# Two output layers and the second feed-forward layer with a 512-column matmul and halves added on VectorE

## Chip, core and metric

The kernel runs on one core of a Trainium2 chip, in one launch. The metric is the device time of a run in microseconds (us). Three runs of the kernel before took 2256.59, 2255.11 and 2259.27 us; the median is 2256.59 us. Engines are called as in the profile: PE is TensorE's matmul (PEld its weight load), DVE is VectorE, ACT is ScalarE, POOL is GpSimd, SP is SyncE, which issues nearly all DMAs.

## What is computed

Three blocks follow each other on x, with 256 tokens and width 1024, in float32. Cut to what matters:

```
x = x + gt1 * (concat(fourier, recurrent) @ w_out)         # block 1: "out1"
x = x + gt2 * experts(...)                                 # 16 experts, 554 MB of weights
x = x + gate * ((attn + gated unit) @ w_out_2)             # block 2: "out2"
x = x + gate2 * (relu(h @ w_ff1_2)**2 @ w_ff2_2)           # block 2: ff1 (1024 to 4096), ff2 (4096 to 1024)
two layers of block 3, each: in3 (1024 to 4096), attention and convolution, out3 (1024 to 1024)
```

Between these stand norms over the features, whose sums over x must be complete before the next layer's results can be scaled.

## The kernel before, in words

All activations lie feature-major: 128 features on the partitions, 8 chunks of them for width 1024, 256 tokens in the free dimension. A dense layer is a list of blocks; one block is one chunk of 128 output features, summed over all input chunks k in one PSUM bank. For accuracy each float32 product is made of three matmuls in the type float32r: high weight by high input, low weight by high input, high weight by low input (`parts`, line 719). Each has 128 input rows, 128 output features and 256 columns (the tokens), and all three add up in the same 256 columns of the bank. out1 and out2 have 8 blocks of 8 chunks (192 matmuls each), ff2 has 8 blocks of 32 chunks (768 matmuls), which go in 32 steps of 8 chunks, each step with its own slice of weights.

The high and low weights are made on the way, one 128-feature slice ("split", 8 chunks of 128 columns) at a time: ACT copies the slice with rounding into one of four places of w_hi (`high_parts`, line 1232, instruction at line 1243), DVE subtracts it from the original and writes ring_lo (`low_parts`, line 1637, instruction at line 1644). A place of w_hi is free again when PE has finished the step that used it. PE's block waits for the count w_split that DVE raises.

The first unit of a layer (three blocks) is computed with k as the outer loop (`k_outer`, line 724, matmuls at line 736), so that PE can begin when the first chunk of input is split; the three blocks end together. The others run one block after the other (line 785); ff2 has its own loop (line 1195).

The results of out1, out2 and ff2 are taken from PSUM by DVE (`update`, line 1828): one scalar_tensor_tensor per block, X = X + gate * PSUM, which raises the count evacuated. PE waits for this count before it reuses a bank, ACT before it squares or rounds the new X. DVE's program is one list in fixed order. In out1 a turn of it is: update of block i, low part of split i+3, sum of squares (line 1765). In out2: update, low part of split i+3, low part of the new X for the next layer (`raise_low`, line 1773), sum of squares. In ff2 a turn without a result is: low part of split i+3 and, up to turn 23, one piece of the modulation product of 1024 columns (`add_third`, lines 1740 and 1743); turns 9 to 11, 21 to 23, 30 and 31 also have update, raise_low and two sums (lines 1750 or 1753, and 1765). The low part of split i+3 thus stands behind update i, and the last splits of these turns are the first three of the next layer.

`link` on DVE (line 1623) lets an instruction raise a count and makes DVE wait for it before the next one.

Of the kernel before, what the change touches and what calls it, by code (L numbers as in the profile page):

```python
# [10 lines left out]
ALU = mybir.AluOpType  # L11
# [3 lines left out]
P = 128  # L15
T = 256
NT = T // P
D = 1024
# [219 lines left out]
def build(nc, inp, scratch, out):  # L238
# [51 lines left out]
    with ctx:  # L290
# [173 lines left out]
        FF_LO = ff_parts[:, 0:8 * K1].rearrange("p (k t) -> p k t", k=FF // P)  # L464
        FF_HI = ff_parts[:, 8 * K1:16 * K1].rearrange("p (k t) -> p k t", k=FF // P)

        U_HI = u_hi.rearrange("p (k t) -> p k t", k=KD)
        U_LO = u_lo.rearrange("p (k t) -> p k t", k=KD)
        R = rs[:, 0:UCOL]
# [173 lines left out]
        def _(pe):  # L643
# [77 lines left out]

                return (hi, x_hi), (lo, x_hi), (hi, x_lo)

            def k_outer(g, lo, src, first, ready, each, order):

                for it in g["items"]:
                    pe.wait_ge(S("w_split"), it["s"] + 1)
                    if it["b"] >= 4:
                        pe.wait_ge(S("evacuated"), it["free"])
                for n, k in enumerate(order):  # L730
                    pe.wait_ge(S(ready), first + n + 1)
                    for i, it in enumerate(g["items"]):
                        x = [a[:, k, :] for a in src(it)]
                        wl = lo[:, k, it["col"]:it["col"] + P]
                        for j, (w, a) in enumerate(parts(w_hi[:, it["s"] % HI, k, :], wl, *x)):
                            m = pe.matmul(ps[:, it["bank"], 0:a.shape[-1]], w, a, start=(n == 0 and j == 0),  # L736
                                          stop=(n == KD - 1 and j == 2), skip_group_check=True)
                        if n == KD - 1:
                            count(m, "unit_used" if it["last"] else "block_done")
                        each(n, i)  # L740
# [6 lines left out]
                count(m, "block_done")  # L747

            def dense_blocks(units, src, first, after=lambda i: None, ready="x_split", each=lambda k, i: None,
                             order=range(KD)):  # L750


                for gi, g in enumerate(units):
                    lo = slot(g["u"], KD, g["w"], of=ring_lo)
                    if gi == 0:
                        k_outer(g, lo, src, first, ready, each, order)
                        first = None
                        for it in g["items"]:
                            if it["last"]:
                                after(gi)  # L760
                            yield
                        continue
                    for it in g["items"]:
                        if "flip" in it:
                            flip(it, out_by(units, {"v": 11, "vs": 19}[it["flip"]]))
                            yield
                            continue
                        pe.wait_ge(S("w_split"), it["s"] + (2 if it["turned"] else 1))
                        if it["b"] >= 4:
                            pe.wait_ge(S("evacuated"), it["free"])  # L770
                        bank = it["bank"]
                        h = src(it)
                        i = it["s"] % HI
                        for t in range(NT if it["turned"] else 1):
                            for k in range(KD):
                                if it["turned"]:
                                    x = [a[:, k, P * t:P * t + P] for a in h]
                                    for j, (w, a) in enumerate(parts(w_hi[:, i:i + 2, k, :], lo[:, k, :], *x)):
                                        m = pe.matmul(ps[:, bank, 2 * P * t:2 * P * t + 2 * P], a, w,
                                                      start=(k == 0 and j == 0), stop=(k == KD - 1 and j == 2))  # L780
                                else:
# [10 lines left out]
            def dense(units, order=range(KD)):  # L792
                for _ in dense_blocks(units, lambda it: (X_HI, X_LO), split_input(), order=order):
                    pass

            inputs_split = [0]
# [181 lines left out]
            for t in range(NT):  # L978
                m = pe.matmul(ps[:, 4 + t, :], ones, ROOTS[:, HEADS * t:HEADS * t + HEADS, :], start=True, stop=True)
            count(m, "o_spread")  # L980
            dense(out1)


            column_sums(False)
# [184 lines left out]
            for g in proj2:  # L1169
                unit_ready(g["u"])  # L1170
                w = slot(g["u"], 2, 4, g["w"])
                for it in g["items"]:
# [4 lines left out]
                        m = pe.matmul(ps[:, it["b"] % 4, 0:T], w[:, it["src"], k, it["col"]:it["col"] + P],  # L1177
                                      (AO, SGO)[it["src"]][:, k, :], start=(k == 0), stop=(k == 3))
                    count(m, "unit_used" if it["last"] else "block_done")
            dense(out2)  # L1180
            for _ in raised_dense(ff1, False):
                pass
            for i, g in enumerate(ff2):
                for b, u in enumerate(g["us"]):
                    lo = slot(u, KD, g["w"], of=ring_lo)
                    pe.wait_ge(S("ff_split"), KD * (b + 1))
                    for it, (_, s) in zip(g["items"], g["at"][b]):
                        pe.wait_ge(S("w_split"), s + 1)
                        if b == 0:
                            pe.wait_ge(S("evacuated"), it["b"] - 3)  # L1190
                        for k in range(KD):
                            wl = lo[:, k, it["col"]:it["col"] + P]
                            x = FF_HI[:, KD * b + k, :], FF_LO[:, KD * b + k, :]
                            for j, (w, a) in enumerate(parts(w_hi[:, s % HI, k, :], wl, *x)):
                                m = pe.matmul(ps[:, it["b"] % 4, 0:T], w, a, start=(b == 0 and k == 0 and j == 0),  # L1195
                                              stop=(b == FF // D - 1 and k == KD - 1 and j == 2), skip_group_check=True)
                        count(m, plan.splits[s]["done"][0])
                    if 4 * i + b == KD + 1:
                        ada_sum(5, ACC, "third_used", THIRDS * KD)
                    if 4 * i + b == KD + 2:  # L1200
                        turn(5)
# [418 lines left out]
        def _(dve):  # L1620
# [207 lines left out]
            def update(it, gate):  # L1828

                waits(*it["done"])  # L1830
                dve.scalar_tensor_tensor(X[:, it["n"], :], ps[:, it["b"] % 4, 0:T], gate[:, it["n"]:it["n"] + 1],
                                         X[:, it["n"], :], ALU.mult, ALU.add).then_inc(S("evacuated"), 1)

            def residual(units, gate):

# [561 lines left out]
```

## Time and profile before

| what | value |
|---|---|
| runs | 2256.59, 2255.11, 2259.27 us |
| span of the profiled execution | 2251.4 us; no time of its own is given beside the span |
| PE / PEld busy | 1827.7 us (81%) / 1151.7 us (51%) |
| DVE / ACT busy | 798.3 us (35%) / 525.3 us (23%) |
| mean granted TensorE clock | 0.780 |
| chain of waits, by engine | DMA 52%, PE 38%, DVE 7%, issue 1%, ACT 1% |
| out1: 192 matmuls | about 255 to 279 us |
| experts | about 322 to 1586 us |
| out2: 192 matmuls | about 1747 to 1771 us |
| ff1 | about 1773 to 1867 us |
| ff2: 768 matmuls | about 1867 to 1958 us |

The busy shares are means over stages that have different limits. The chain of waits is followed back from the last instruction, and each of its pieces says from when, for how long and which instruction held the end. A clock of 1.00 is 2.4 GHz, 0.50 is 1.2 GHz.

### The profile page before, as it was taken

The page shows a single profiled execution, that of the slowest core. Times are in us where ns is not written, and L with a number is a line of the kernel's source. Part 1 is how long each engine was busy: PE and PEld are TensorE (multiplying, and loading weights), DVE is VectorE, ACT ScalarE, POOL GpSimd, SP SyncE. Part 2 cuts the span into 40 slices and gives each one's busy share as a digit, 9 for nine tenths or more (in the row PEclk, how much of TensorE's full clock was granted, in tenths as well). Part 3 has the DMA queues.
Part 4 walks back from the last instruction along what each step waited for, and adds up shares of the span by engine and source line. Part 5 has one row for each costly group of instructions (what it writes and reads, how often), then busy time and mean ns, then how long its engine had stood idle before and what let it go on. Part 6 is the DMA issues. An engine that isn't in the chain of part 4 may idle for free.

```text
span 2251.4 us, 33931 instructions
## 1 busy us (share of the span) xinstructions
PE 1827.7 (81%) x14864; PEld 1151.7 (51%) x14864; DVE 798.3 (35%) x1237; ACT 525.3 (23%) x857; POOL 52.6 (2%) x85
## 2 busy tenths in 40 slices
PE   5999887777777776677777777667899999999897
PEld 4896752312222221221221222221798999998897
DVE  5666630000000000000000000010775788688777
ACT  2420220000000000000000000000574564365664
POOL 0024000000000000000000000000000000000000
PEclk9999986657656656765665675675899999999998
DMA  9877899999999999999999999999744559853541
GB/s 368 295 283 292 345 410 425 424 426 425 425 426 425 425 426 425 426 426 426 424 426 426 425 426 425 426 425 425 242 152 138 169 177 348 279 169 122 169 132 66
DMA packets 161044, 760.62 MB, mean 338 GB/s; under 512 B 10391, under 2 KB 99223, under 8 KB 109368
## 3 DMA queue, kind: packets, MB, share of 16 engines
q1 hardware_dynamic: 157288, 754.07, 83.9%
q10 hardware_dynamic: 3664, 5.24, 0.7%
q8 instruction: 68, 1.11, 0.2%
q14 instruction: 24, 0.20, 0.0%
HBM read 756.13 MB, written 3.14 MB: 337 GB/s over the span
## 4 chain that ended last, share of the span: by engine, by line
DMA 52%; PE 38%; DVE 7%; issue 1%; ACT 1%; SPq 0%; DVEq 0%; ACTq 0%
DMA arena<-in_w_exp_gate 22%; DMA arena<-in_w_exp_up 21%; PE ps L785 17%; PE ps L1195 4%; DMA ring<-in_w_exp_down 3%; PE ps L1053 3%; PE ps L736 3%; DMA arena<-in_w_ada 2%; PE ps L1067 2%; DMA ring<-in_w_exp_up 2%; PE ps L659 1%; DVE ring_lo L1644 1%; PE ps L1177 1%; PE ps L931 1%; DVE const L2027 1%
## 5 line engine op out<-in xcount | busy, mean ns | idle before, releaser
L1053 PE MATMUL ps<-arena,const 128*32 128x352 f32 x2816 | 409.1, 726 | 162.4 <-DMA arena<-in_w_exp_gate 100.7
L1053 PEld LDWEIGHTS ps<-arena,const 128*32 128x32 f32 x2816 | 99.1, 148 | 460.0 <-DMA arena<-in_w_exp_gate 181.3
L1644 DVE TENSOR_TENSOR ring_lo<-ring,w_hi 128x1024 fp32r<-128x1024 f32 x220 | 267.4, 1219 | 45.8 <-ACT w_hi L1243 44.8
L785 PE MATMUL ps<-u_hi,w_hi 128*128 128x258 f32 x960 | 275.5, 287 | 1.3 <-DVE ring_lo L1644 1.1
L2025 DVE TENSOR_TENSOR tail<-tail,ps 128x704 f32<-128x704 f32 x15 | 13.3, 888 | 742.1 <-PE ps L1053 742.1
L785 PE MATMUL ps<-u_hi,ring_lo 128*128 128x258 f32 x960 | 271.2, 282 | 0.0
L785 PE MATMUL ps<-u_lo,w_hi 128*128 128x258 f32 x960 | 271.0, 282 | 0.0
L1243 ACT ACTIVATE w_hi<-ring 128x1024 fp32r<-128x1024 f32 x220 | 230.2, 1050 | 74.3 <-PE ps L1195 30.5
L1053 PE MATMUL ps<-ring,const 128*32 128x352 f32 x1024 | 159.4, 773 | 49.0 <-DMA ring<-in_w_exp_up 36.7
L785 PEld LDWEIGHTS ps<-u_hi,w_hi 128*128 128x128 f32 x960 | 181.6, 189 | 7.3 <-issue 5.2
L785 PEld LDWEIGHTS ps<-u_lo,w_hi 128*128 128x128 f32 x960 | 181.7, 189 | 0.0
L785 PEld LDWEIGHTS ps<-u_hi,ring_lo 128*128 128x128 f32 x960 | 181.2, 189 | 0.0
L1067 PE MATMUL ps<-ring,const 128*32 128x256 f32 x1536 | 120.0, 455 | 63.5 <-DMA ring<-in_w_exp_down 63.5
L2029 DVE TENSOR_TENSOR arena<-arena,ps 128x2048 f32<-128x2048 f32 x15 | 34.3, 2288 | 372.0 <-PE ps L1081 372.0
L1053 PEld LDWEIGHTS ps<-ring,const 128*32 128x32 f32 x1024 | 37.7, 155 | 170.4 <-DMA ring<-in_w_exp_up 90.8
L1067 PE MATMUL ps<-arena,const 128*32 128x256 f32 x896 | 85.8, 528 | 45.9 <-DVE const L2027 42.5
L1426 ACT ACTIVATE const<-ps 128x256 f32<-128x256 f32 x16 | 6.1, 384 | 482.4 <-PE ps L1022 482.4
L1421 ACT ACT_TABLE_LOAD x15 | 19.2, 1283 | 408.5 <-PE ps L1053 408.5
L785 PE MATMUL ps<-x_parts,w_hi 128*128 128x256 f32 x592 | 107.4, 280 | 5.4 <-DVE ring_lo L1644 5.4
L1067 PEld LDWEIGHTS ps<-ring,const 128*32 128x32 f32 x1536 | 49.0, 123 | 111.3 <-DMA ring<-in_w_exp_down 79.6
L785 PEld LDWEIGHTS ps<-x_parts,w_hi 128*128 128x128 f32 x592 | 91.4, 188 | 7.6 <-DVE ring_lo L1644 7.1
L1195 PE MATMUL ps<-ff_parts,w_hi 128*128 128x256 f32 x512 | 88.2, 277 | 0.0
(287 smaller groups left out, 2359.3 us busy)
## 6 DMA issues: line engine op xcount, KB each, us to landing
arena<-in_w_exp_gate SPq DMA_DIRECT2D x96, 1408.0 KB, 35.3
arena<-in_w_exp_up SPq DMA_DIRECT2D x80, 1408.0 KB, 36.5
ring<-in_w_exp_down SPq DMA_DIRECT2D x64, 1536.0 KB, 38.0
ring<-in_w_exp_up SPq DMA_DIRECT2D x48, 1408.0 KB, 35.3
ring<-in_w_in SPq DMA_DIRECT2D x37, 1536.0 KB, 7.0
arena<-in_w_exp_down SPq DMA_DIRECT2D x32, 1536.0 KB, 35.3
ring<-in_w_ada SPq DMA_DIRECT2D x24, 1536.0 KB, 8.8
ring<-in_w_ff SPq DMA_DIRECT2D x18, 1536.0 KB, 7.3
```

The lines of the kernel that those rows point to most:

```text
L659: m = pe.matmul(ps[32 * j:32 * j + 32, 6 + i, 0:ADA_J // 2], conds[:, kc, :], slot(u, ADA_PASS)[:, at:at + ADA_J // 2], start=(kc == 0), s ...
L736: m = pe.matmul(ps[:, it["bank"], 0:a.shape[-1]], w, a, start=(n == 0 and j == 0), stop=(n == KD - 1 and j == 2), skip_group_check=True)
L785: m = pe.matmul(ps[:, bank, 0:a.shape[-1]], w, a, start=(k == 0 and j == 0), stop=(k == KD - 1 and j == 2))
L931: m = pe.matmul(o[:, :, half, :], KG[:, 4 * d + h, P * t:P * t + P], r[:, :, half, :], start=True, stop=True, skip_group_check=True)
L1053: m = pe.matmul(ps[32 * j:32 * j + 32, 2 * (k // 8) + i, 0:FJ // 2], XCUR[:, k % 8, :], SLOT[s][:, at:at + FJ // 2], start=(k % 8 == 0), s ...
L1067: m = pe.matmul(ps[32 * j:32 * j + 32, 4, 0:T], HIDT[:, c, :], SLOT[s][:, at:at + T], start=(c == 0), stop=(c == FC - 1), skip_group_check ...
L1177: m = pe.matmul(ps[:, it["b"] % 4, 0:T], w[:, it["src"], k, it["col"]:it["col"] + P], (AO, SGO)[it["src"]][:, k, :], start=(k == 0), stop= ...
L1195: m = pe.matmul(ps[:, it["b"] % 4, 0:T], w, a, start=(b == 0 and k == 0 and j == 0), stop=(b == FF // D - 1 and k == KD - 1 and j == 2), s ...
L1243: mark(act.activation(w_hi[:, s % HI, :, :], slot(c["u"], KD, c["w"])[:, :, c["col"]:c["col"] + P], ACT.Copy), "w_high")
L1644: tt(slot(c["u"], KD, c["w"], of=ring_lo)[:, :, at], slot(c["u"], KD, c["w"])[:, :, at], w_hi[:, s % HI, :, :].bitcast(F32), ALU.subtract) ...
L2027: dve.transpose(HIDT, HID.rearrange("p (q c) -> p c q", c=FC)).then_inc(S("hid_t"), 1)
L2029: tt(moe, moe, ps[:, 4:8, :], ALU.add).then_inc(S("acc_done"), 1)
```

## The change

In out1, out2 and ff2 the two products with the high weight become one matmul of 512 columns: the high weight meets the high and the low input, which lie behind each other in memory (views X_BOTH and FF_BOTH), and the output fills the whole PSUM bank, one half for each. The product of the low weight and the high input still has 256 columns and adds to the half of the high input (half 0 in out1 and out2, half 1 in ff2, where the low part lies first). The two halves are added into X by DVE, with two scalar_tensor_tensor instead of one; the first is linked, and the second raises evacuated. The other layers (in1, in2, ff1, in3, out3) keep three matmuls of 256 or 258 columns.

```diff
+        X_BOTH = x_parts.rearrange("p (s k t) -> p s k t", s=2, k=KD)
+        FF_BOTH = ff_parts.rearrange("p (s k t) -> p s k t", s=2, k=FF // P)
+            def two_products(bank, hi, lo, both, k, of_hi, first, last):
+                out = ps[:, bank, :].rearrange("p (s t) -> p s t", s=2)
+                pe.matmul(out, hi, both[:, :, k, :], start=first, stop=False, skip_group_check=True)
+                return pe.matmul(out[:, of_hi, :], lo, both[:, of_hi, k, :], start=False, stop=last, skip_group_check=True)
...
+                        if both is not None:
+                            m = two_products(it["bank"], w_hi[:, it["s"] % HI, k, :], wl, both, k, 0, n == 0, n == KD - 1)
...
-            dense(out1)
+            dense(out1, both=X_BOTH)
...
-            dense(out2)
+            dense(out2, both=X_BOTH)
...
-                            x = FF_HI[:, KD * b + k, :], FF_LO[:, KD * b + k, :]
-                            for j, (w, a) in enumerate(parts(w_hi[:, s % HI, k, :], wl, *x)):
-                                m = pe.matmul(ps[:, it["b"] % 4, 0:T], w, a, start=(b == 0 and k == 0 and j == 0),
-                                              stop=(b == FF // D - 1 and k == KD - 1 and j == 2), skip_group_check=True)
+                            m = two_products(it["b"] % 4, w_hi[:, s % HI, k, :], wl, FF_BOTH, KD * b + k, 1,
+                                             b == 0 and k == 0, b == FF // D - 1 and k == KD - 1)
...
             def update(it, gate):
                 waits(*it["done"])
-                dve.scalar_tensor_tensor(X[:, it["n"], :], ps[:, it["b"] % 4, 0:T], gate[:, it["n"]:it["n"] + 1],
-                                         X[:, it["n"], :], ALU.mult, ALU.add).then_inc(S("evacuated"), 1)
+                link(stt(X[:, it["n"], :], ps[:, it["b"] % 4, 0:T], gate[:, it["n"]:it["n"] + 1], X[:, it["n"], :],
+                         ALU.mult, ALU.add), "first_half")
+                stt(X[:, it["n"], :], ps[:, it["b"] % 4, T:2 * T], gate[:, it["n"]:it["n"] + 1], X[:, it["n"], :],
+                    ALU.mult, ALU.add).then_inc(S("evacuated"), 1)
```

## Rows read from the trace of the kernel before

**Rows 1.** The page, part 4: chain of waits by line, share of the span.
```profile
DMA arena<-in_w_exp_gate 22%; DMA arena<-in_w_exp_up 21%; PE ps L785 17%; PE ps L1195 4%; DMA ring<-in_w_exp_down 3%; PE ps L1053 3%; PE ps L736 3%; DMA arena<-in_w_ada 2%; PE ps L1067 2%; DMA ring<-in_w_exp_up 2%; PE ps L659 1%; DVE ring_lo L1644 1%; PE ps L1177 1%; PE ps L931 1%; DVE const L2027 1%
```

**Rows 2.** Chain of waits, out2: start us, us, what.
```profile
1746.95 7.79 PE ps L736 x66
...
1756.53 14.41 PE ps L785 x120
...
1770.96 0.49 DVE X L1831
...
1772.94 8.21 PE ps L736 x66
```

**Rows 3.** Chain of waits, out1 and the update behind it.
```profile
264.69 14.42 PE ps L785 x120
...
279.13 0.50 DVE X L1831
```

**Rows 4.** Chain of waits, end of ff2 and first unit of in3.
```profile
1954.97 0.48 DVE X L1831
...
1957.73 0.48 DVE X L1831
...
1959.71 9.70 PE ps L736 x66
```

**Rows 5.** Busy time in windows: length, PE, PEld, DVE, ACT, POOL (instructions), clock, DMA, GB/s.
```profile
1755.00:1772.00 17.00, 14.82 (x124) 14.41 (x122) 16.53 (x29) 12.88 (x23) 0.00 (x0) 1.00 0.58 186
1867.00:1943.00 76.00, 76.00 (x672) 76.00 (x672) 71.61 (x85) 34.61 (x42) 0.00 (x0) 1.00 0.95 343
```

**Rows 6.** Timeline of PE: start us, us, instruction, shapes, count.
```profile
177.59 3.68 PE L931 MATMUL ps<-arena 128*128 128x64 f32 x32
...
1593.79 0.42 PE L736 MATMUL ps<-u_lo,w_hi 128*128 128x258 f32 x1
1594.00 0.42 PE L736 MATMUL ps<-u_hi,w_hi 128*128 128x258 f32 x1
...
2097.03 0.70 PE L816 MATMUL ps<-arena,const 128*128 128x256 f32 x2 [0.93 <-DVE arena L1765]
```

**Rows 7.** Timeline of DVE in out1 and out2.
```profile
256.79 0.49 DVE L1982 SCALAR_TENSOR_TENSOR arena<-arena,vec 128x256 f32<-128x256 f32 x1
257.31 0.29 DVE L1687 CAST x_parts<-arena 128x256 fp32r<-128x256 f32 x1
...
261.57 0.43 DVE L1678 TENSOR_TENSOR x_parts<-arena,x_parts 128x256 fp32r<-128x256 f32 x1
...
1754.86 0.48 DVE L1831 SCALAR_TENSOR_TENSOR X<-ps,mod,X 128x256 f32<-128x256 f32 x1 [4.88 <-PE ps L736]
1755.26 1.21 DVE L1644 TENSOR_TENSOR ring_lo<-ring,w_hi 128x1024 fp32r<-128x1024 f32 x1
...
1756.78 0.48 DVE L1831 SCALAR_TENSOR_TENSOR X<-ps,mod,X 128x256 f32<-128x256 f32 x1
...
1759.04 0.48 DVE L1831 SCALAR_TENSOR_TENSOR X<-ps,mod,X 128x256 f32<-128x256 f32 x1
```

**Rows 8.** Timeline of DVE in ff2; in brackets the idle time before, and its releaser.
```profile
1894.47 0.48 DVE L1831 SCALAR_TENSOR_TENSOR X<-ps,mod,X 128x256 f32<-128x256 f32 x1 [1.74 <-PE ps L1195]
...
1905.56 1.22 DVE L1644 TENSOR_TENSOR ring_lo<-ring,w_hi 128x1024 fp32r<-128x1024 f32 x1
...
1927.11 0.48 DVE L1831 SCALAR_TENSOR_TENSOR X<-ps,mod,X 128x256 f32<-128x256 f32 x1 [0.49 <-PE ps L1195]
...
1938.67 3.49 DVE L1644 TENSOR_TENSOR ring_lo<-ring,w_hi 128x1024 fp32r<-128x1024 f32 x3
```

**Rows 9.** Windows of 1 us for the granted clock, the column after POOL.
```profile
1771.00:1772.00 1.00, 0.00 (x0) 0.00 (x0) 1.00 (x2) 0.52 (x2) 0.00 (x0) 1.00 0.48 173
1960.00:1961.00 1.00, 1.00 (x7) 1.00 (x6) 1.00 (x3) 0.45 (x1) 0.00 (x0) 0.54 0.93 304
2100.00:2101.00 1.00, 0.00 (x0) 0.00 (x0) 0.96 (x3) 0.00 (x0) 0.00 (x0) 0.51 1.05 389
```

More of the change, by code:

```diff
@@ L722, in parts, with k_outer @@
                 return (hi, x_hi), (lo, x_hi), (hi, x_lo)
-            def k_outer(g, lo, src, first, ready, each, order):
+            def two_products(bank, hi, lo, both, k, of_hi, first, last):
+                out = ps[:, bank, :].rearrange("p (s t) -> p s t", s=2)
+                pe.matmul(out, hi, both[:, :, k, :], start=first, stop=False, skip_group_check=True)
+                return pe.matmul(out[:, of_hi, :], lo, both[:, of_hi, k, :], start=False, stop=last, skip_group_check=True)
+            def k_outer(g, lo, src, first, ready, each, order, both):
                 for it in g["items"]:
@@ L732, in k_outer @@
                     for i, it in enumerate(g["items"]):
-                        x = [a[:, k, :] for a in src(it)]
                         wl = lo[:, k, it["col"]:it["col"] + P]
-                        for j, (w, a) in enumerate(parts(w_hi[:, it["s"] % HI, k, :], wl, *x)):
-                            m = pe.matmul(ps[:, it["bank"], 0:a.shape[-1]], w, a, start=(n == 0 and j == 0),
-                                          stop=(n == KD - 1 and j == 2), skip_group_check=True)
+                        if both is not None:
+                            m = two_products(it["bank"], w_hi[:, it["s"] % HI, k, :], wl, both, k, 0, n == 0, n == KD - 1)
+                        else:
+                            x = [a[:, k, :] for a in src(it)]
+                            for j, (w, a) in enumerate(parts(w_hi[:, it["s"] % HI, k, :], wl, *x)):
+                                m = pe.matmul(ps[:, it["bank"], 0:a.shape[-1]], w, a, start=(n == 0 and j == 0),
+                                              stop=(n == KD - 1 and j == 2), skip_group_check=True)
                         if n == KD - 1:
@@ L749, in dense_blocks @@
             def dense_blocks(units, src, first, after=lambda i: None, ready="x_split", each=lambda k, i: None,
-                             order=range(KD)):
+                             order=range(KD), both=None):
                 for gi, g in enumerate(units):
@@ L755, in dense_blocks @@
                     if gi == 0:
-                        k_outer(g, lo, src, first, ready, each, order)
+                        k_outer(g, lo, src, first, ready, each, order, both)
                         first = None
@@ L780, in dense_blocks @@
                                                       start=(k == 0 and j == 0), stop=(k == KD - 1 and j == 2))
+                                elif both is not None:
+                                    m = two_products(bank, w_hi[:, i, k, :], lo[:, k, it["col"]:it["col"] + P], both, k, 0,
+                                                     k == 0, k == KD - 1)
                                 else:
@@ L790, in dense_blocks, with dense @@
                         yield
-            def dense(units, order=range(KD)):
-                for _ in dense_blocks(units, lambda it: (X_HI, X_LO), split_input(), order=order):
+            def dense(units, order=range(KD), both=None):
+                for _ in dense_blocks(units, lambda it: (X_HI, X_LO), split_input(), order=order, both=both):
                     pass
```

## Prediction

> **What bounds the kernel now.** First the chain of waits by line: 43% of the span is DMA of expert weights [rows 1], which the change doesn't touch. The changed layers are PE lines 736 and 785 in part and line 1195 (4%). Next the chain of waits in order of time, around each changed layer [rows 2 to 4]. The reader is to see that inside a layer it runs over PE, but at both joints over DVE: from the end of the first unit over update and low part to the next block, and from the last update over the low part to the first unit of the next layer. The windows [rows 5] say how much room DVE has: in out2 it is busy 16.53 of 17.00 us, more than PE with 14.82; in ff2 it is busy 71.61 of 76 us beside a PE without a gap. So PE is the bound in ff2 by a little, DVE nearly is one already, and in out2 DVE is the fuller engine. The change takes time from PE and gives time to DVE.
>
> **PE: what two matmuls instead of three are worth.** A matmul of 256 columns costs (14.41 - 0.17 of tail) / 120 = 0.119 us in out1 and out2 [rows 2, 3] and 76.00 / 672 = 0.113 us in ff2 [rows 5]. So one k costs 0.356 us there and 0.339 us in ff2. At half clock, 258 columns follow each other at 0.21 us [rows 6]: one column in a cycle of 1.2 GHz. At 2.4 GHz 256 columns alone would be 0.107 us. What holds them at 0.113 to 0.119 shows in the 64-column matmuls, each with its own weights: 3.68 / 32 = 0.115 us with a quarter of the columns [rows 6]. I read that as a floor per pair of weight load and matmul. The profile before has no float32r matmul of 512 columns, so it is bounded from both sides: 0.213 us if only columns count, 0.238 us if it costs twice the 256-column one. I take 0.216, as its length covers the next weight load, and the low-weight matmul stays at its pace. Then one k is 0.335 us (0.021 less) in out1 and out2 and 0.329 (0.010 less) in ff2, between nothing and, if only columns count, 0.036 and 0.019 less. Over 128 and 256 k that is 2.7 + 2.6 = 5.3 us of PE time, between 0 and 9.5.
>
> The Trainium skill, "TensorE: Matmul & The Clock Gate", section "Back-to-back issue gap", puts a lone matmul at N / 2.4 GHz plus 2.5 ns. For 256 columns that is 0.109 us, and the trace disagrees with 0.113 to 0.119. For 512 columns it gives 0.216 us, which no row here shows. By it one k would go from 0.328 to 0.325 us, and PE would save 1 us in all.
>
> **DVE: what the second add costs.** An update's instruction lasts 0.48 us, and where the next one doesn't wait for its end it takes 0.40 us of DVE's time: in the first turn of out2 from 1754.86 to 1755.26. The linked form is in the trace as well: a scalar_tensor_tensor of the same shape starts at 256.79, the next instruction at 257.31, so 0.52 us [rows 7]. The new update is 0.52 + 0.40 = 0.92 us: 0.52 more, 24 times. It can't be less than 0.40 more, as the second one is of the same form. PE and ACT wait for the second one, since evacuated moves to it; behind it stands the low part of split i+3. The Trainium skill, "Trainium Kernel Development and Optimization", section "Best Practices", warns that tiling speeds up TensorE but not the emptying of PSUM. The update row agrees in so far as each half has to be read at the full 0.48 us; by this rule alone the change costs DVE 24 times one update.
>
> **out1.** The first unit doesn't get shorter: DVE splits the last input chunk until 262.00 [rows 7], and nine matmuls at 0.119 are left (1.07 us), or three k at 0.335 (1.0). Then update 0 and split 3 stand on the path: +0.52. Five blocks of 8 k: -0.84 [rows 3]. DVE's turn, out2's 2.26 without the 0.40 of raise_low, becomes 1.86 + 0.52 = 2.4 us against a block of 2.68, so it keeps up. The last update stands on the path to the column sums: +0.52. Sum +0.2 us, between -0.4 (columns alone count) and +1.0 (no gain). It reaches the end only through the top-k and the slots that PE frees for the experts, so zero is possible too; I take 0.2.
>
> **out2.** The first unit ends at E = 1746.95 + 7.79 = 1754.74, in the new kernel 24 x 0.021 = 0.5 us earlier. From there all 8 turns of DVE's list lie ahead, and only 5 blocks of PE. Before: update 0 at E + 0.12, one turn of 1.92 (no sum of squares) and turns of 2.26 [rows 7]; without waiting update 7 would come at E + 15.6, and it comes at E + 16.22 [rows 2], when block 7 is done. DVE had 0.6 us to spare in the whole layer. Now the turns are 2.44 and 2.78: update 7 at E' + 0.12 + 2.44 + 6 x 2.78 = E' + 19.24. PE begins block 3 at E' + 2.3 and ends block 7 at E' + 2.3 + 5 x 2.68 = E' + 15.7. PE's gain is lost in front of DVE. From update 7 to ff1's first matmul took 1.98 us [rows 2] and takes 2.50. Together 3.02 + 0.52 - 0.5 = +3.0 us, between +2.6 (first unit by columns alone) and +3.5 (no gain).
>
> **The clock behind out2.** PE is now idle from E' + 15.7 to E' + 21.7, 6.0 us, where it was 2.0 us. After 2.0 us idle the clock was still 1.00 in one place (1771) and 0.54 in another (1960) [rows 9]; PE's column sums end at 2097.73 [rows 6], and at 2100 the clock is 0.51 [rows 9]. So 6 us nearly surely ends in 1.2 GHz at the start of ff1. The same first unit took 8.21 us from a warm start and 9.70 from a mostly cold one [rows 2, 4], 1.5 us more. Its end is on the path, as ACT's next high part and the roots wait for it. I take +1.6, between 0 (no drop) and 2.1, if it begins wholly cold.
>
> **ff2.** In turn 9 DVE waits 1.74 us for PE, in turn 21 0.49 [rows 8]: the updates of turns 9 to 11 make it late, the turns 12 to 20 (2.34 us each against a block of 2.72) bring it back. From update 9 to the end of split 27's low part it takes 1938.67 + 1.22 - 1894.47 = 45.42 us, of which 0.49 is waiting. Block 27 begins five blocks after the end of block 21, 1927.08 + 5 x 2.72 = 1940.7, and split 27 is ready at 1939.9: 0.8 us to spare. Now ten blocks of 8 x 0.010 bring update 9 forward by 0.8, to 1893.7. Six longer updates and no wait give 45.42 - 0.49 + 3.12 = 48.05 us, and split 27 is ready at 1941.7. So PE stalls, in short pieces from split 15 on, and block 27 begins 1.0 us later than before although each block is shorter. Four more blocks give back 0.3. Between the last two updates DVE had 2.76 us of work [rows 4] for a block of 2.72; now 3.28, and then the last update is itself longer: +1.04. Sum +1.7 us. It is +2.8 without a gain per k. At the other end DVE's 1.74 us of waiting is all that can be won before turn 9: +0.4. The idle PE at the end of ff2 already leads into 1.2 GHz, so that costs nothing more. SP issues thirds of the modulation weights when DVE has used earlier ones; those come up to 5 us later, with DMA busy 0.95 of this window [rows 5], which can only speak for later.
>
> **Sum.** 0.2 + 3.0 + 1.6 + 1.7 = +6.5 us on the span of 2251.4, so 2257.9. The profile gives its execution no time beside the span; I add the 5.2 us by which the median of the runs, 2256.59, stands over it: 2263.1 us. After these joints the chain is PE and DVE to the end without a DMA, so nothing gives the delay back.
>
> **Rivals.** (a) The clock stays up behind out2: 2261.5 us. For it speaks only the place at 1771, whose gap was a third as long. (b) The 512-column matmul costs twice the 256-column one, so PE gains nothing: out1 +1.0, out2 +3.5, ff2 +2.8, clock +1.6, in all +8.9, 2265.5 us. (c) The clock falls in the longer gap behind the first unit of out1 as well (2.3 us instead of 1.8): 1.5 us more, 2264.6. (d) Faster: DVE absorbs the second add. Then PE's 5.3 us show in full, less 0.52 at five joints: -2.7, 2253.9 us. That decides at DVE's turn in out2: eight turns must fit into 2.3 + 13.4 us, which needs a turn of 2.27 us, and the one before is 2.26 with a single add. In the profile nothing speaks for it but the low mean share of DVE, 35%, which is a mean over the experts' stage.
>
> **How the numbers follow.** Chances: forecast 0.45, (a) 0.25, (b) 0.15, (c) 0.09, (d) 0.06. 0.2% is 4.5 us, about what a measurement can tell from no change here, so slower means over 2261.1. The forecast lies 2 us above that, the runs before spread over 4 us: I count 0.38 of its 0.45, 0.14 of (a) and all of (b) and (c) as slower: 0.76. Same 0.18, faster 0.06. The bounds add up to between +2.6 and about +11 us, 2259.2 to 2267.7; with the spread of the runs, and a little to the side of (d), 2257.5 to 2268.5.
>
> **What would show it.** Right: in out2 DVE has no wait between update 0 and update 7, at turns of 2.8 us; PE idles about 6 us in front of ff1 and its first unit takes 9.5 us or more; in ff2 waits of PE on line 1644 that were not there; line 1195's pair takes 0.33 us per k. Wrong: turns of 2.3 us in out2, a gap in front of ff1 near 2 us, or ff2's matmuls ending earlier than 90 us after their start.

## The result and the profile after

The changed kernel takes 2272.87 us (median of 9 runs; 2268.35 to 2277.62, and one disturbed run of 2777.95 us that is left out of the ratio). The kernel before takes 2259.27 us in the 9 runs shared with it. The ratio is 1.0056 [1.004, 1.0073], so 12.7 us slower (9 to 16.5). Forecast was slower by 6.5 us, 2263.1 us, with 2268.5 at the upper end: the direction is right, the size half of what came, and the time lies above the range.

Part 4 of the page after, the chain of waits by line. Against [rows 1] the PE lines of the changed layers (731 and 732, once 1195 and parts of 736 and 785) hold 5%, and the low part of VectorE (1658, once 1644) 2% instead of 1%.

```profile
DMA arena<-in_w_exp_up 22%; DMA arena<-in_w_exp_gate 22%; PE ps L801 18%; DMA ring<-in_w_exp_down 3%; PE ps L1069 3%; PE ps L731 3%; PE ps L749 3%; PE ps L1083 2%; DMA ring<-in_w_exp_up 2%; PE ps L732 2%; DVE ring_lo L1658 2%; PE ps L662 1%
```

Chain of waits in order of time, out2, after (start us, us, what); it answers to [rows 2].

```profile
1759.46 0.50 DVE X L1845
1759.98 0.48 DVE X L1847
1760.46 0.61 DVE ring_lo L1658
...
1778.66 0.41 DVE X L1845
1779.09 0.48 DVE X L1847
1779.57 1.14 DVE ring_lo L1658
...
1781.07 10.73 PE ps L749 x66
```

Before, the chain ran 14.41 us over PE between the first and the last update. Now it doesn't touch PE from 1759.46 to 1781.07 (VectorE's last update starts at 1778.58 in its timeline; the chain counts it from 1778.66). The timeline of DVE, against [rows 7], says why: update in two instructions, low part, raised low, sum of squares, and the next update at once (1761.91 to 1764.69 is a turn of 2.78 us).

```profile
1761.91 0.48 DVE L1845 SCALAR_TENSOR_TENSOR X<-ps,mod,X 128x256 f32<-128x256 f32 x1
1762.42 0.48 DVE L1847 SCALAR_TENSOR_TENSOR X<-ps,mod,X 128x256 f32<-128x256 f32 x1
1762.82 1.22 DVE L1658 TENSOR_TENSOR ring_lo<-ring,w_hi 128x1024 fp32r<-128x1024 f32 x1
1763.95 0.48 DVE L1787 SCALAR_TENSOR_TENSOR u_lo<-X,cols,u_hi 128x256 fp32r<-128x256 f32 x1
1764.35 0.42 DVE L1779 TENSOR_TENSOR arena<-arena 128x256 f32<-128x256 f32 x1
1764.69 0.48 DVE L1845 SCALAR_TENSOR_TENSOR X<-ps,mod,X 128x256 f32<-128x256 f32 x1
```

Timeline of PE in ff2, after. The nine starts of the 512-column matmul from 1881.23 to 1884.06 make eight steps of 0.354 us: 0.236 for it, 0.118 for the 256-column one.

```profile
1881.23 0.40 PE L731 MATMUL ps<-ff_parts,w_hi 128*128 128x512 f32 x1
1881.47 0.28 PE L732 MATMUL ps<-ff_parts,ring_lo 128*128 128x256 f32 x1
1881.58 0.40 PE L731 MATMUL ps<-ff_parts,w_hi 128*128 128x512 f32 x1
...
1884.06 0.40 PE L731 MATMUL ps<-ff_parts,w_hi 128*128 128x512 f32 x1
```

Windows after: length, then PE, PEld, DVE, ACT, POOL (instructions), clock, DMA share, GB/s. The first answers to [rows 5]: a PE without a gap in both, but 431 matmuls in 76 us make 0.3527 us per k, where 672 made 0.3393. (A window also counts the matmuls that reach into it at its edges; by starts it is 0.353 against 0.340.) The second and third answer to [rows 9]: PE idles from 1776.05 to 1781.07, the clock is still 1.00 between 1 and 2 us into that gap, and ff1 begins at 0.50.

```profile
1878.00:1954.00 76.00, 76.00 (x431) 65.90 (x430) 71.07 (x88) 33.32 (x41) 0.00 (x0) 1.00 0.92 329
...
1777.00:1778.00 1.00, 0.00 (x0) 0.00 (x0) 1.00 (x2) 1.00 (x3) 0.00 (x0) 1.00 0.74 157
1781.00:1784.00 3.00, 2.93 (x14) 2.96 (x14) 1.63 (x3) 0.37 (x1) 0.00 (x0) 0.50 0.41 151
```

Timeline of DVE in ff2, after; it answers to [rows 8] (updates of turns 9 and 21, and the end of split 27's low part, the first of four that are put together at 1953.34).

```profile
1906.17 0.48 DVE L1845 SCALAR_TENSOR_TENSOR X<-ps,mod,X 128x256 f32<-128x256 f32 x1 [2.08 <-PE ps L732]
...
1940.22 0.48 DVE L1845 SCALAR_TENSOR_TENSOR X<-ps,mod,X 128x256 f32<-128x256 f32 x1 [0.34 <-PE ps L732]
...
1953.34 4.62 DVE L1658 TENSOR_TENSOR ring_lo<-ring,w_hi 128x1024 fp32r<-128x1024 f32 x4
```

Chain at the end of ff2, after [rows 4]. PE takes the end over at 1954.62, as soon as split 27 is ready: it had waited 0.3 us for it, its only wait for a low part within ff2. The last two updates end 3.17 us apart, where it was 2.76.

```profile
1953.42 1.15 DVE ring_lo L1658
1954.62 0.50 PE ps L731
...
1969.26 0.50 DVE X L1845
1969.78 0.48 DVE X L1847
...
1972.95 0.48 DVE X L1847
...
1974.93 9.52 PE ps L749 x66
```

The stages of all profiles, in us, from starts in PE's timeline: out1 from its first matmul to its column sums, out2 to ff1's first matmul, ff1's first unit to its first block, ff2 to in3's first matmul. The last column is when out1 begins; up to there all these programs are the same.

| kernel | out1 | out2 | ff1's first unit | ff2 | out1 begins |
|---|---|---|---|---|---|
| before | 25.7 | 26.3 | 9.2 | 92.7 | 254.9 |
| e1_same_kernel | 26.0 | 26.4 | 10.7 | 92.7 | 257.7 |
| after | 26.9 | 29.9 | 11.7 | 97.2 | 259.5 |
| e2_double_add | 26.4 | 29.4 | 11.1 | 95.2 | 260.0 |
| e3_pairs_one_add | 26.0 | 26.2 | 10.7 | 95.6 | 262.0 |
| f5_out_only | 26.9 | 29.8 | 11.1 | 92.7 | 260.5 |
| f6_ff2_only | 26.0 | 26.4 | 9.2 | 97.2 | 260.7 |
| f7_add_out2 | 25.5 | 29.4 | 10.5 | 92.7 | 269.1 |
| f8_split_ahead | 24.7 | 25.6 | 10.7 | 92.7 | 267.1 |
| f9_after_ahead | 25.7 | 29.2 | 10.9 | 97.3 | 261.0 |

Spans of single executions don't compare well here, as out1 begins anywhere from 254.9 to 269.1 us in equal code, and before's was the earliest. The two spans differ by 14.7 us: 4.6 ahead of out1, 1.2 in out1, -1.2 from its end to in2, 3.5 in out2, 2.5 in ff1's first unit, 4.6 in ff2 and -0.5 behind it. So stages are compared, and ratios over many runs.

### The profile page after: what moved, and what is told of

The parts are those of the page before. It is cut to its first block, busy times and chain, and to the rows that moved or that the text cites. A ratio compares the mean times of both kernels' runs of the same rounds, so it can differ in the third digit from the quotient of the medians.

```text
span 2266.1 us, 33187 instructions
## 1 busy us (share of the span) xinstructions
PE 1834.5 (81%) x14480; PEld 1143.3 (50%) x14480; DVE 809.6 (36%) x1261; ACT 525.0 (23%) x857; POOL 52.6 (2%) x85
## 4 chain that ended last, share of the span: by engine, by line
DMA 50%; PE 40%; DVE 8%; ACT 1%; issue 1%; SPq 0%; DVEq 0%; ACTq 0%
DMA arena<-in_w_exp_up 22%; DMA arena<-in_w_exp_gate 22%; PE ps L801 18%; DMA ring<-in_w_exp_down 3%; PE ps L1069 3%; PE ps L731 3%; PE ps L749 3%; PE ps L1083 2%; DMA ring<-in_w_exp_up 2%; PE ps L732 2%; DVE ring_lo L1658 2%; PE ps L662 1%; PE ps L1193 1%; PE ps L947 1%; DVE const L2043 1%
## 5 line engine op out<-in xcount | busy, mean ns | idle before, releaser
L731 PE MATMUL ps<-ff_parts,w_hi 128*128 128x512 f32 x256 | 91.0, 399 | 0.3 <-DVE ring_lo L1658 0.3
L1279 ACT ACTIVATE arena<-tail 128x256 f32<-128x256 f32 x116 | 58.4, 509 | 103.3 <-DVE tail L1828 102.8
L801 PE MATMUL ps<-x_parts,w_hi 128*128 128x256 f32 x432 | 79.5, 281 | 3.1 <-DVE ring_lo L1658 3.1
```

Of the source, the lines that this page charges most:

```text
L731: pe.matmul(out, hi, both[:, :, k, :], start=first, stop=False, skip_group_check=True)
L1279: mark(act.activation(dst, TMP[:, it["b"] % 3, 0:T], func, scale=scale, bias=TMP[:, it["b"] % 3, at:at + 1]), "evacuated")
```

## Experiments

Theory A: the second add makes VectorE's list the bound in out2 and, in part, in ff2, and the 512-column matmul gives PE nothing. Theory B: the pair gives what was forecast, and something else costs. The expectations call by A, B and so on what each of them states itself, which is not always these two.

**e1_same_kernel**: the kernel before, under another name.

> The kernel before, unchanged, against itself: ratio 1.000 in both theories. It shows how much of the difference between the two profiles before out1 (4.6 us) and of the pace of the 256-column matmuls (0.113 us in parts of one profile, 0.118 us in the same code of the other) comes and goes without any change. Theory A (pace is a state of the execution): this profile has other stretches at 0.113 and 0.118 than the first. Theory B (the changed kernel slows them): the same stretches are at 0.113 again.

Ratio 0.9999 [0.9987, 1.0011]. Its stages are those of before but for 0.3 us in out1 and for ff1's first unit, 10.7 us against 9.2 with the same 2.0 us of idle PE ahead: part of that term comes by chance. The paces bear out its theory A: 30 us of in1 at full clock hold 267 matmuls in the profile before (100 to 130) and 257 in e1 (103 to 133), edges included; by starts that is 0.113 and 0.118 us each, in the same code.

**e2_double_add**: three matmuls as before, and the second instruction of the update on the same half, times 0.0.

```diff
-                dve.scalar_tensor_tensor(X, ps[..., 0:T], gate, X, mult, add).then_inc(S("evacuated"), 1)
+                link(stt(X, ps[..., 0:T], gate, X, mult, add), "first_half")
+                stt(X, ps[..., 0:T], 0.0, X, mult, add).then_inc(S("evacuated"), 1)
```

> Three 256-column matmuls as before, but each update on VectorE is two linked instructions (the second adds 0.0 times the same half). Theory A (VectorE's list is the whole loss): ratio 1.0040 to 1.0060 (+9 to +13 us), out2 about 3 us longer, the gap in front of ff1 near 6 us with a fall of the clock behind it, ff2 2 to 3 us longer. Theory B (the 512-column matmul is to blame as well, by 3.7 us in ff2): ratio 1.002 to 1.0035.

Ratio 1.0042 [1.0027, 1.0057], +9.5 us. The longer add alone lengthens out2 by 3.0 and ff2 by 2.5 us against e1, and the ratio lies where theory A of this expectation put it. It is a little less than the change's own add: with the constant 0.0 in place of the gate the second instruction lasts 0.42 us and not 0.48, and a turn of out2 takes 2.72 us (1760.54 to 1763.25) and not 2.78. Over eight turns that is the 0.5 us by which out2 is shorter here, and in f7, than in the changed kernel.

**e3_pairs_one_add**: the pair of matmuls, but one add, which reads only the half that the low weight went to; the product of high weight and the other half of the input is left out of the result.

```diff
-            def update(it, gate):
+            def update(it, gate, half=0):
-                ... ps[:, it["b"] % 4, 0:T] ...
+                ... ps[:, it["b"] % 4, half * T:half * T + T] ...
```

> The two matmuls of the change, but one update instruction, which reads only the half with the high input; the product of high weight and low input is computed and left out of the result. Theory A: ratio 0.999 to 1.001, no longer gap in front of ff1. Theory B: the pair of matmuls at 0.353 us instead of 0.339 costs ff2 3.7 us, ratio 1.001 to 1.002. As first predicted (a pair is 0.010 to 0.021 us shorter) it would be 0.9975 to 0.9985.

Ratio 1.001 [0.9998, 1.0022], +2.3 us. out2 stays at 26.2 us: PE's pair saves nothing there. ff2 gets 2.9 us longer with a DVE that does no more than before. Windows of ff2 of e2 (first) and e3 (second): PE of e2 has short waits, PE of e3 none, and yet 410 matmuls make 0.351 us per k, edges included. So neither theory holds alone. In out2 the second add is the whole loss. In ff2 both cost: the add of e2 alone 2.5 us, the pair alone 2.9, and the change 4.6, so they overlap in part; there the pair's loss is what theory B of both expectations named.

```profile
1877.00:1949.00 72.00, 71.39 (x628) 71.06 (x627) 68.09 (x86) 31.83 (x39) 0.00 (x0) 1.00 0.95 339
```

```profile
1877.00:1949.00 72.00, 72.00 (x410) 62.53 (x409) 65.92 (x78) 31.46 (x38) 0.00 (x0) 1.00 0.91 328
```

**e4_pace**: series of matmuls of one width each, every one with its own weights, nothing else running; the output is a copy of x, and nothing of the reference is computed.

```python
for cols in (64, 128, 192, 256, 320, 384, 448, 512):
    for i in range(64):
        pe.matmul(ps[:, i % 4, 0:cols], w[:, P * (i % 8):P * (i % 8) + P], x[:, 256 * (i % 4):256 * (i % 4) + cols], start=True, stop=True)
```

> Not the kernel's computation: it copies x to the output and runs series of independent matmuls, each with its own weight load, of 64 to 512 columns, in float32r and float32, first with no DMA, then beside one. Theory A (a float32r column costs 0.46 ns, no floor is met at 256): 0.118 us at 256, 0.177 at 384, 0.236 at 512, and from 192 columns down the floor of the weight load near 0.11. Theory B (floor of weight load plus matmul at 0.113 to 0.119 as predicted): 192 and 256 columns cost the same, 512 costs 0.216 when it stands alone.

Timeline of PE (start, us, instruction, count), at full clock:

```profile
23.83 4.44 PE L62 MATMUL ps<-mov,wr 128*128 128x64 f32 x39
...
57.73 5.44 PE L62 MATMUL ps<-mov,wr 128*128 128x256 f32 x44
...
74.76 8.48 PE L62 MATMUL ps<-mov,wr 128*128 128x384 f32 x48
...
100.80 10.59 PE L62 MATMUL ps<-mov,wr 128*128 128x512 f32 x46
```

A pace is the length without the last matmul, by one less than the count: 64 columns 0.112 us, 256 columns (5.44 - 0.28) / 43 = 0.120, 384 columns 0.173, 512 columns (10.59 - 0.39) / 45 = 0.227. The 192-column series has 0.112 too, so there is a floor up to there, and 256 columns already stand above it: each 128 more cost 0.053. Of the expectation A's floor came out and B's equal cost of 192 and 256 columns did not; 0.227 at 512 lies between A's 0.236 and B's 0.216. With DMA traffic beside them (DMA share 1.01) 256 and 512 columns come out the same, 0.120 and 0.227. The Trainium skill, "TensorE: Matmul & The Clock Gate", section "Back-to-back issue gap", gives 216 ns for a lone 512-column matmul and 131 ns as a sustained pace with its weight load; no run here shows either, the trace has 227.

**f10_pace_pair**: the pair and the three, accumulating in blocks of 8 k as in the kernel.

> Matmuls alone, with weights and accumulation as in the kernel, blocks of 8 k over four PSUM banks; the output is a copy of x, nothing of the reference is computed. Series: three matmuls of 256 columns per k, the pair 512 and 256, 512 alone in one view of the bank and in two halves, 256 accumulating and each on its own. Theory: the pair's pace is a matter of the matmuls alone, so 0.353 us per k comes out here too, three matmuls give 0.340 to 0.360, 512 alone 0.227 as in the series without accumulation. Rival: accumulation or the split view makes the difference between 0.236 and 0.227; then 512 accumulating is at 0.236. Rival: traffic or other engines in the whole kernel make it; then the pair takes 0.347 here.

Timeline of PE: the pair, then 512 columns alone in one view of the bank (L82) and in two halves (L87).

```profile
49.40 0.40 PE L78 MATMUL ps<-mov,wr 128*128 128x512 f32 x1
49.64 0.28 PE L79 MATMUL ps<-mov,wr 128*128 128x256 f32 x1
...
58.94 0.40 PE L78 MATMUL ps<-mov,wr 128*128 128x512 f32 x1
...
66.71 10.81 PE L82 MATMUL ps<-mov,wr 128*128 128x512 f32 x47
77.36 4.92 PE L87 MATMUL ps<-mov,wr 128*128 128x512 f32 x21
```

The pair's starts at 49.40 and 58.94 are 27 k apart: 0.353 us, the kernel's pace with nothing else running. 512 alone stays at 0.227 in either view, and three matmuls take 0.360. So the wide matmul takes 0.009 us more where it alternates with 256 columns; accumulation and the view don't add that here, nor does DMA traffic (e4, and a second series of the pair in f10 beside it, at 0.353 again). Why alternation does stays open. Against 0.356 us (out1, out2) the pair gains 0.003 per k, against the 0.339 of ff2 it loses 0.013.

**f5_out_only** and **f6_ff2_only**: the change in out1 and out2 alone, and in ff2 alone.

```diff
+            def update(it, gate, both=True):      # f6: both=False, and the calls the other way round
-                            update(it, mod[:, 3, 16:24])
+                            update(it, mod[:, 3, 16:24], False)
```

> The change in out1 and out2 alone; ff2 keeps three matmuls and one add. Theory A (the VectorE list is the loss, the pair gains nothing there): blocks of out1 and out2 at 0.353 us per k; out2 from its first to ff1's first matmul 29.9 us (before 26.3, +3.5), out1 +1.0, ff1's first unit 1.5 to 2.5 us longer than from a warm start, ff2 92.6 us as before. Sum +6.5 us against before, ratio 1.003. Rival B (most of the change's 12.7 us sits in ff2, and the pair pays in the output layers): ratio 1.0015 or less, out2 at most 28.5 us. Rival C (the later start of in1 and out1 in the changed kernel's profile, 45.0 against 42.1 us, comes with the changed program and not by chance): in1 starts near 45 us here as well, and 3 us come on top.

> The change in ff2 alone; out1 and out2 keep three matmuls and one add. Theory A: ff2, from its first to in3's first matmul, takes 97.2 us as in the full change (before 92.6), out2 26.3 us, ff1's first unit as before. Sum +4.6 us, ratio 1.002. Rival B: ff2 is longer only because it starts later and its transfers of thirds fall elsewhere; then here, with its start as before, it takes 95 us or less and the ratio is under 1.001.

f5: 1.0038 [1.0027, 1.005], +8.6 us. f6: 1.0017 [1.0003, 1.0032], +3.8 us. The sum is 12.4 of 12.7. In each the touched stages have the lengths of the full change and the others those of before, so each loss is local: rival B of f6 falls, as ff2 takes 97.2 us though out2 and ff1's first unit ahead of it are as before. Rival C of f5 falls too: in1 starts at 45.1 us in f7 and at 46.4 in f8, whose code is that of before up to out1. In f5 the stages show 0.9 + 3.4 + 1.1 = 5.4 us, where ff1's unit is counted by means (below), and the interval of the ratio begins at 6.1 us; that is not accounted for. The profiled execution was the fastest of f5's ten.

**f7_add_out2**: the longer add in out2 alone, three matmuls everywhere (the two instructions of e2's update, at out2's call only).

> Three matmuls everywhere; the second instruction of the update (here it adds 0.0 times the same half, same shape) in out2 alone. Theory A: VectorE's turns in out2 are 2.78 us, out2 takes 29.4 us (+3.0), ff1's first unit 10.7 to 11.7 us instead of 9.1 (clock at its lower level, 1.2 GHz), ff2 as before. Sum +5 us, ratio 1.002. Rival D (the first unit is slow as often in the kernel before, so the longer gap adds nothing): ff1's first unit over several profiles of before is near 10.7 as well, and the ratio is 1.0013.

Ratio 1.0007 [0.9992, 1.0022]; out2 29.4 us and ff2 as before. The stage confirms A, with turns of 2.72 us where it said 2.78. The ratio (1.6 us, -1.8 to 5.0) holds the stages' 3.0 + 1.1 us and just reaches the forecast of 5, but stands as near to D's 1.0013 as to no change, so it decides nothing. Rival D is partly right: the same first unit of ff1 behind out2 with one add took 9.2, 10.7, 10.7 and 9.2 us (before, e1, e3, f6; mean 9.9), with two adds 11.7, 11.1, 11.1, 10.5 and 10.9 (after, e2, f5, f7, f9; mean 11.1). The granted clock goes with it: with one add, after 2.0 us of idle PE, it stayed 1.00 in before and f6 and fell to 0.50 in e1 and e3; with two adds, after 4.6 to 5.4 us, the unit began at 0.50 all five times. The two groups overlap, so their difference of 1.1 us rests on few profiles.

**f8_split_ahead**: the kernel before, with the fourth low part of out1 and out2 ahead of the first update.

```diff
             def residual(units, gate):
+                low_parts(units[0]["items"][0]["s"] + HI)
...
             waits("x_normed", KD)
+            low_parts(starts["out2"] + HI)
```

> The kernel before, with the low part of the fourth weight block of out1 and out2 made ahead of the first update instead of behind it. Theory A (this low part stands on the path at both joints): PE's gap between the first unit and the first block falls from 1.3 us to under 0.2 us in out1 and out2, both layers get 1.2 us shorter, ratio 0.999. Rival E: in out2 VectorE's list is the bound in any order, so only out1 gets shorter and the ratio is 0.9995 or more. Rival F: in out1 the low part delays the first update more than it brings, no change.

Ratio 0.9985 [0.9971, 0.9999], 3.4 us faster. out1 is 1.3 us shorter than in e1, out2 0.7. Chain of waits in out2:

```profile
1763.55 0.49 DVE X L1831
...
1764.88 0.96 ACT w_hi L1243
1765.87 1.23 DVE ring_lo L1644
...
1779.51 1.14 DVE ring_lo L1644
...
1781.00 9.66 PE ps L736 x66
```

PE's gap behind the first unit is gone, but then the chain runs over DVE to the end: with room of 0.6 us in its list, out2 can't give more. Rival E holds in half.

**f9_after_ahead**: the same two lines in the changed kernel. (In the expectations of f9, f11 and g13 the gap of 5.3 us counts from the start of out2's last matmul; by the trace's idle time it is 5.0.)

> The changed kernel, with the low part of the fourth weight block of out1 and out2 made ahead of the first update. Theory A (in out2 VectorE's list is the bound from the first update on): the list gets 1.1 us shorter, so out2 takes 28.7 us instead of 29.9 although PE's blocks start 1.8 us earlier; PE's gap in front of ff1 grows from 5.3 to about 6 us; out1 2.0 us shorter; together 3 us less than the changed kernel, ratio to before 1.0042. Rival B (PE's start of the fourth block is what counts): out2 28.0 us or less.

Ratio 1.0034 [1.0014, 1.0054], which is less than the changed kernel's but not clear of it. out1 is 1.3 us shorter (forecast 2.0), out2 0.6 (29.2 us, forecast 28.7). PE's first block begins at once, but a later one waits 0.7 us for its low part; PE ends only 1.0 us earlier in the layer, and its idle time in front of ff1 grows from 5.0 to 5.4 us: the list decides, as A has it. In its timeline it is one low part (1.13 us) shorter, but the first raised low now waits 0.58 us for ACT; that is the half us that the forecast missed.

```profile
1757.90 0.48 DVE L1845 SCALAR_TENSOR_TENSOR X<-ps,mod,X 128x256 f32<-128x256 f32 x1 [3.42 <-PE ps L732]
...
1759.48 0.49 DVE L1787 SCALAR_TENSOR_TENSOR u_lo<-X,cols,u_hi 128x256 fp32r<-128x256 f32 x1 [0.58 <-ACT u_hi L1285]
```

**f11_after_warm** and **f12_ahead_warm**: matmuls without use in front of first units, behind all waits for split weights: f11 the changed kernel (20 before ff1), f12 the kernel of f8 (28 before in2, 14 before ff1, in3, out3).

```diff
+                i = g["items"][0]["s"] % HI
+                for n in range(20 if g is ff1[0] else 0):
+                    pe.matmul(ps[:, g["items"][0]["bank"], 0:T] ..., w_hi[:, i, n % KD, :], w_hi[:, i, 0:2, :],
+                              start=True, stop=True, skip_group_check=True)
                 for n, k in enumerate(order):
                     pe.wait_ge(S(ready), first + n + 1)
```

> The changed kernel, with 20 matmuls of 256 columns without use on PE between out2 and ff1, as soon as ff1's first three weight blocks are split. Theory A (the 5.3 us gap brings TensorE to 1.2 GHz and ff1's first unit pays for it): no half clock at the start of ff1, the first unit 9.2 us instead of 11.7, 2 us less than the changed kernel, ratio to before 1.005. Rival B: the 20 matmuls start late, run at the lower level and last 4.3 us, so ff1 begins later and nothing is won. Rival C: the first unit is long because it waits for the last of VectorE's raised input, whatever the clock: 10.5 us or more at full clock.

> The kernel before with both measures: the fourth low part of out1 and out2 ahead, and matmuls without use on PE in the gaps in front of the first units of in2 (28), ff1, and both in3 and out3 (14 each). Theory A: first units go from 10.5 to 11 us down to 9.2 in in2, ff1 and both in3, and by 0.9 us in both out3; with e8's 3 us (interval 0.2 to 6.6) together 8 us less than before, ratio 0.9965. Rival B: the useless matmuls stand in the way at joints where PE is released early, and the ratio stays at 0.9985 as in the kernel with the low parts alone.

f11 1.0057 [1.0038, 1.0075], f12 1.0016 [0.9998, 1.0034]: rival B both times, and f12 is worse than the 0.9985 that its B named. In f12 ff1 begins 27.3 us after out2 and in3 94.8 after ff2, where it was 25.6 and 92.7 in f8. PE timeline of f11: the series comes after 4.91 us of idling, released by the third low part, runs at half clock (0.50 from 1779 to 1783) and lasts 4.61 us. ff1 begins 34.2 us after out2, 4.3 later than in the changed kernel, and its first unit, 9.8 instead of 11.7 us, gives back less than that.

```profile
1779.01 4.61 PE L742 MATMUL ps<-w_hi 128*128 128x256 f32 x20 [4.91 <-DVE ring_lo L1662]
```

**g13_warm_early** and **g14_ahead_warm**: the same, behind the waits of the first weight block only. g13 is the changed kernel with 42, g14 the kernel of f8 with 20 in front of ff1, 16 in front of the first in3 and both out3, 30 in front of the second in3, and none in front of in2.

```diff
                 for it in g["items"]:
                     pe.wait_ge(S("w_split"), it["s"] + 1)
                     if it["b"] >= 4:
                         pe.wait_ge(S("evacuated"), it["free"])
+                    if it is g["items"][0]:
+                        for n in range(42 if g is ff1[0] else 0):
+                            pe.matmul(ps[:, it["bank"], 0:T] ..., w_hi[:, it["s"] % HI, n % KD, :], w_hi[:, it["s"] % HI, 0:2, :], ...)
```

> The changed kernel with 42 matmuls of 256 columns without use on PE in front of ff1, released by the first weight block of ff1, so right behind out2's last block. Theory A (the gap of 5.3 us costs the clock at ff1's start): PE is busy through the gap, the granted clock stays 1.00, ff1 begins 29.9 us after out2 as in the changed kernel, and its first unit takes 8.7 us to the column sums, as at full clock in f11_after_warm, instead of 11.7: 2 to 3 us less, ratio to before 1.0045. Rival B: the first matmuls of the series wait too, run at 1.2 GHz and delay ff1, no gain, ratio 1.0055. Rival C: the unit is held by VectorE's raised input, 9.5 us or more at full clock, ratio 1.005.

> The kernel before with the fourth low part of out1 and out2 ahead, and matmuls without use released by the first weight block of the next layer in front of ff1 (20), in3 (16 and 30) and out3 (16 each). Theory A: no half clock at these joints, first units from 10.65 to 8.9 (ff1), 9.5 and 11.2 to 8.7 (in3), 9.65 to 8.55 (both out3), with no delay of their start: 6 us less than with the low parts alone, ratio to before 0.996. Rival B: a released series runs past the point at which its layer is ready and gives the gain back: 0.9985.

PE timeline of g13, and a window of it:

```profile
1773.67 5.19 PE L742 MATMUL ps<-w_hi 128*128 128x256 f32 x42
1778.73 0.36 PE L754 MATMUL ps<-u_hi,w_hi 128*128 128x258 f32 x1
```

```profile
1780.00:1783.00 3.00, 3.00 (x27) 3.00 (x26) 0.41 (x1) 0.00 (x0) 0.00 (x0) 1.00 0.04 14
```

g13: 1.003 [1.0014, 1.0046]. ff1 begins 29.7 us after out2, as in the changed kernel, at clock 1.00, and its first unit takes 9.2 us instead of 11.7. (The 11.7 in the expectations of f11 and g13 is to the first block; to the column sums it was 10.6, in g13 8.0.) The ratio fell by 0.0026, 6 us, more than this stage gives, but its interval holds the 2.5 us too. So the lower level costs the changed kernel 2.5 us here, and 1.1 us more than the kernel before on the mean of the profiles, where the clock falls at times too. Rivals B and C fall. g14: 0.9971 [0.9954, 0.9987], 2252.34 us, 6.6 us faster than the kernel before and the fastest of all kernels here. Its interval and that of f8 overlap, so what the useless matmuls add to the early low parts is shown by the clock and the stages, not by the ratio. Its windows at the starts of ff1 and in3, at full clock:

```profile
1775.00:1783.00 8.00, 8.00 (x69) 8.00 (x68) 1.74 (x3) 0.48 (x1) 0.00 (x0) 1.00 0.50 175
...
1962.00:1970.00 8.00, 8.00 (x68) 7.97 (x67) 1.79 (x3) 0.59 (x2) 0.00 (x0) 1.00 1.05 355
```

## Why the prediction was right in direction and too small

**PE's pair: failed.** "I take 0.216, as its length covers the next weight load": it is 0.236 us in the pair (f10), and 0.227 even among its own kind. The reading behind it failed as well: the floor is 0.112 us, seen up to 192 columns, and the 256-column matmul already stands above it (e4). With nothing else running the pair saves 0.360 - 0.353 = 0.007 us per k (f10), a third of the 0.021 that I counted in out1 and out2. Rival (b), "costs twice the 256-column one", was right for out1 and out2 (0.353 against 0.356 us per k). In ff2 it is worse than any end that I gave: I put the worst case at no gain, though my own bound of 0.238 beside the 0.113 of ff2 makes 0.351 and so a loss of 0.012. It was a loss of 0.013 per k, as the pair has one pace everywhere and the three matmuls of ff2 ran at 0.113 instead of 0.119.

**DVE's second add: right.** It takes 0.52 us more of a turn (2.78 instead of 2.26; from 1761.91 to 1762.42, the linked half, is 0.51).

**out1: +0.2, measured +0.9 (against e1) to +1.2.** Two updates of 0.52 stand on the path, as written; the -0.84 of five blocks didn't come.

**out2: +3.0, measured +3.5.** The mechanism came out as written: update 0 at 1759.46 and update 7 at 1778.58 are 19.12 us apart, where the forecast had 19.12, and VectorE has no wait between. Missing was only the 0.5 us by which the first unit was to get shorter.

**Clock behind out2: +1.6.** The fall came, at a clock of 0.50. The gap was 5.0 us where I had 6.0: counted from the end of the first unit, ff1 began at E' + 21.7 as forecast, but without the gain per k PE ended at E' + 16.7 instead of E' + 15.7. Against the profile shown the fall costs 2.5 us, on the mean of nine profiles 1.1. What I missed is that the level after 2.0 us of idling is chance already in the kernel before.

**ff2: +1.7, measured +4.6.** VectorE's path was right: from update 9 to the end of split 27's low part 1954.57 - 1906.17 = 48.40 us with 0.34 of waiting, so 48.06 of work; forecast 48.05. But update 9 comes 1.05 us later in the layer (28.47 against 27.42 us after its start) where 0.8 us earlier was forecast, for the pace of PE. That moves block 27 by 1.9 us, and the four last blocks cost 0.4 instead of giving 0.3: 1.7 + 1.9 + 0.7 = 4.3. The one wrong number is 2.6 us here. The short waits of PE that I expected from split 15 on didn't come, as PE itself was slower; there was one, of 0.3 us, at split 27.

**The base.** These executions take 2.3 us more than their span (2268.35 against 2266.1; 2255.67 against 2253.4 in e1). The 5.2 us that I added left 2.9 for the luck of the profiled execution, which was reasonable. But the three runs shown had a median 2.7 us below the nine that the change was timed with.

**Sum.** 2272.87 is 9.8 us above the forecast: 2.7 of base, 2.9 in ff2, 1.2 in out1 and out2 (against e1), less 0.5 at the clock (1.1 on the mean, where I had 1.6). The rest, 3.5 us, is within the ratio's interval of 3.8 to either side; f5 says that if it is real, it comes with out1 or out2. The range was too narrow: it held the loss of PE's gain as one rival, without a loss in ff2, and the spread of the base's median not at all. The +12.7 us stand above even the +11 that its bounds added up to.

## What to carry to other kernels

Merging two matmuls that share weights need not save PE time when each of them is already wide enough to stand above the floor of a narrow one (here 0.112 us up to 192 columns, 0.120 at 256); measure the pace of the exact pair first (here 0.353 us per k against 0.339 to 0.356). It costs time on the engine that empties PSUM, so count that engine's whole list between two updates against one block: in out2 it had 0.6 us to spare in eight turns. Idle PE in front of a layer costs once more where the clock falls (up to 2.5 us in ff1's first unit), and matmuls without use fill such a gap only if they are not held back by the wait that ends it.

## What the runs showed of the hardware

256-column float32r matmuls had three paces at full clock, 0.113, 0.118 and 0.120 us, and 0.113 or 0.118 in the same code in different executions (out1's blocks: 13.60 us for 119 steps in e2 and f7, 0.114; 0.119 before). In ff2 the three matmuls ran at 0.113 in all eight profiles that have them there, so the pair's loss in ff2 is not chance. Alone, in e4 and f10, they never ran faster than 0.120, also with DMA traffic, so what makes 0.113 possible stays open. A 512-column matmul is slower by 0.009 us beside a 256-column one than among its own kind.
